# Paged keys turned by VectorE in 32x32 blocks instead of by TensorE

## The chip, the core and the metric

The kernel runs on one core of one Trainium2 chip. The metric is the device time of one execution in microseconds (us). All data is float32.

## The reference

One step of a one-layer decoder for a prompt of 512 tokens and for 64 sample tokens (8 sequences of 8). The part that matters here is the sparse attention of the sample tokens. Each sequence has 2048 past positions in 16 pages of 128 keys; a page table says where each page lies in the cache. A page of keys is `128 x 8 heads x 128` floats, 512 KB, and so is a page of values.

```python
phys = jax.vmap(lambda pt, ids: pt[ids])(page_table, pidx // PAGE_SIZE)
k_sel = jnp.where(is_past, cache_k[phys, slot], gather(k, nidx))
logits = jnp.einsum('bthd,btkhd->bthk', q, k_sel) * ATT_SCALE
logits = logits + bias                      # relative position
p = jax.nn.softmax(jnp.where(valid, logits, -inf), axis=-1)
out = jnp.einsum('bthk,btkhd->bthd', p, v_sel)
```

The kernel does not gather single keys: it computes the logits of all 2048 past keys and adds a mask that leaves the 256 chosen ones.

## The kernel before

The program is written by hand for five engines with semaphores. PE (TensorE) multiplies, ACT (ScalarE) and DVE (VectorE) empty PSUM, POOL (GpSimd) helps, and SP (SyncE) issues nearly all loads, in program order, each after the waits that stand ahead of it.

The sample attention lies in the middle of the program. It runs over two groups `G` of four sequences. For each group there are three stages.

- **Keys.** 64 pages, page number `kp` outermost and the sequence `bb` inside, so that four neighbouring pages of the loop are the same `kp` of four sequences. SP loads each page into one of eight slots `ring` (keys on the 128 partitions, 4 KB each, line 711). For the logits the head dimension must lie on the partitions, so PE turns the page by eight 128x128 transposes (line 1197) into two PSUM banks (`kp`); ACT copies one bank into `KTb` (line 1510), DVE the other (line 1793). Then PE multiplies with `QZ`, the queries of one sequence padded to 32 columns (line 1210), and adds up the four sequences in one PSUM tile `kl`. DVE adds bias and mask into `LS` (function `logits`, line 1787).
- **Softmax.** DVE and ACT finish the rows of `LS`, PE transposes the probabilities (line 1229), and they go into `PTs`.
- **Values.** 64 pages, sequence outermost, through the same eight slots; PE multiplies them as they are (line 1245).

Between these, PE computes "side" tiles, column tiles of the input projection which nothing in the attention needs: a tile is 48 matmuls (lines 987 to 989), and every second one makes SP load the next 1 MB chunk of weights, which ACT and DVE split into a high and a low part (lines 1358 and 582). Where each tile stands is set by the tables `SIDE_B`, `SIDE_V` and the calls `put_side`. Before the change: three tiles at `start`, one at each softmax, nine in each value stage, none in the key stages.

The mask of the chosen keys is computed by DVE in `S`. Ahead of the first key stage SP writes it to memory (line 719) and reads it back four times, once for each group of 32 partitions, into `MG` (line 722). These are the only large loads before the change that go to 32 partitions at a time: 32 rows of 8.5 KB each.

Of the kernel before, what the change touches and what calls it, by code (L numbers as in the profile page):

```python
# [19 lines left out]
P = 128  # L20
# [87 lines left out]
def hybrid_kernel(nc, x_prompt, x_sample, cache_k, cache_v, cache_idx_k, state_ffn_conv, page_table, rel_bias,  # L108
# [42 lines left out]
    two, three = {7: 1, 16: 1}, {4: 1, 10: 1, 16: 1}  # L151
    SIDE_V = [two, two, two, three, two, two, three, {4: 1, 10: 1}]
# [8 lines left out]
    put_side(('start',), 3)  # L161
    for G in range(2):
        put_side(('softmax', G, 0), 1)
# [59 lines left out]
    for G in range(2):  # L223
        for n in range(64):
            single.add('kp', G, n, 0)
            single.add('kp', G, n, 1)
        for kp in range(NPG):
            pair.add('kl', G, kp, at=kp % 2)
        for i, tile in enumerate(side_at['softmax', G, 0] + side_at['softmax', G, 1]):
            pair.add(*tile, at=(i + 1) % 2)  # L230
# [3 lines left out]
        for b in range(4):  # L234
            pair.add('o', G, b, at=0)
            for kp in range(NPG):
                for tile in side_at.get(('V', G, b, kp), ()):
                    pair.add(*tile, at=1)
            single.add('ot', G, b, 0)
            single.add('ot', G, b, 1)  # L240
    pair.add(*side[-1], at=1)
# [60 lines left out]
    with ctx:  # L302
# [141 lines left out]
        QZ = R3[:, 4352:6400].rearrange("p (h b c) -> p h b c", h=H, b=8)  # L444
        kTn = blocks(R3[:, 6400:7424], H)
        KTb = [blocks(RB[:, 1024 * i:1024 * i + 1024], H) for i in range(2)]
# [98 lines left out]
        def page_freed(e, seq):  # L545
# [8 lines left out]
            G, kind, n = (seq - 8) // 128, (seq - 8) // 64 % 2, (seq - 8) % 64  # L554
            if kind == 0:
                e.wait_ge(single_filled, single.slots['kp', G, n, 1][0] + 1)
            else:
                e.wait_ge(S_("v_pages_used"), 64 * G + n + 1)
# [66 lines left out]
        def _(sp):  # L625
# [78 lines left out]
            def load_page(seq):  # L704
                if seq >= 256:
                    return
                G, kind, n = seq // 128, seq // 64 % 2, seq % 64
                b, kp = (4 * G + n % 4, n // 4) if kind == 0 else (4 * G + n // 16, n % 16)
                page_freed(sp, seq)
                v = page_id(sp, b, kp)  # L710
                sp.dma_start(ring[seq % 8], (cache_k, cache_v)[kind][0, bass.ds(v, 1)]
                             .rearrange("o p h d -> (o p) (h d)")).then_inc(page_in[seq % 8], 16)

            side_loads('start')
            for seq in range(4):
                load_page(seq)

            sp.wait_ge(S_("sample_mask"), 1)
            sp.dma_start(mask_scr, S).then_inc(S_("mask_out"), 16)
            sp.wait_ge(S_("mask_out"), 16)  # L720
            for j in range(4):
# [1265 lines left out]
```

## Time and profile before

| | us |
|---|---|
| median of 3 runs (lowest, highest) | 1591.89 (1589.79, 1596.37) |
| the profiled execution: its span, first to last instruction | 1593.2 |
| first key stage, from the first transposes to the start of the softmax | 465 to 581 |
| first value stage | 596 to 705 |
| second key stage | 705 to 812 |
| second value stage | 828 to 930 |

A time of its own beside the span is not given for the profiled execution; the span lies within the range of the three runs. A stage's times are read from the timeline of the trace, and from where line 1197, 1245 or 987 begins. A duration of one matmul is longer than its share of the engine's time, since matmuls overlap in the array; so a stage's PE work is read from busy time or from the distance between repeats.

### The profile page before, as it was taken

How to read it: one execution, taken by the hardware profiler on the slowest of the kernel's cores; microseconds unless marked ns; L12 is line 12 of the kernel's file. 1: busy time of each engine (PE TensorE's matmuls, PEld its weight loads, DVE VectorE, ACT ScalarE, POOL GpSimd, SP SyncE). 2: the span in 40 equal slices, each digit the busy share in tenths (PEclk: the TensorE clock that was granted, in tenths of full speed). 3: DMA queues.
4: the chain of work that ended last, by engine and by line, in shares of the span. 5: the costliest groups of instructions: out<-in, count | busy, mean ns of one | idle time of the engine just before them, and what ended most of it. 6: DMA issues, size and time to landing. Idle time of an engine off the chain costs nothing.

```text
span 1593.2 us, 32571 instructions
## 1 busy us (share of the span) xinstructions
PE 1471.7 (92%) x13518; PEld 1334.5 (84%) x13518; DVE 762.0 (48%) x1030; ACT 511.5 (32%) x818; POOL 234.5 (15%) x371
## 2 busy tenths in 40 slices
PE   7999998979979989899998998899799999999995
PEld 4867798957867778797777998799699999999995
DVE  5288699496514540025540135543555555552123
ACT  4243223324323341023341122122344455442121
POOL 3423234154210000000000000321000110000000
PEclk8899999989999999999999999899799999999998
DMA  5415223122159979999869976133322233223221
GB/s 173 149 27 159 65 80 113 57 96 73 49 188 369 332 249 342 383 358 329 310 223 402 363 258 240 34 125 104 113 80 80 80 90 95 83 98 102 79 83 60
DMA packets 179278, 266.58 MB, mean 167 GB/s; under 512 B 20522, under 2 KB 136539, under 8 KB 178043
## 3 DMA queue, kind: packets, MB, share of 16 engines
q1 hardware_dynamic: 167947, 243.95, 44.5%
q0 software_dynamic: 5104, 11.11, 2.1%
q10 hardware_dynamic: 6080, 9.44, 1.6%
q8 instruction: 107, 1.75, 0.4%
q14 instruction: 40, 0.33, 0.1%
HBM read 240.28 MB, written 24.18 MB: 166 GB/s over the span
## 4 chain that ended last, share of the span: by engine, by line
PE 77%; DVE 8%; DMA 5%; ACT 3%; SPq 2%; issue 2%; POOL 2%; ACTq 0%; DVEq 0%
PE PS L987 14%; PE PS L989 13%; PE PS L988 13%; PE PS L1197 8%; PE PS L1210 4%; PE PS L1245 3%; PE PS L1319 3%; PE PS L1318 3%; PE PS L1317 3%; DMA R<-in_cache_v 3%; PE PS L1028 2%; PE PS L1029 2%; PE PS L1030 2%; PE PS L1173 1%; PE PS L1120 1%
## 5 line engine op out<-in xcount | busy, mean ns | idle before, releaser
L987 PE MATMUL PS<-xn_hi,WH 128*128 128x288 f32 (+1 forms) x1424 | 430.7, 302 | 16.0 <-DVE xn_lo L1614 13.2
L988 PE MATMUL PS<-xn_lo,WH 128*128 128x288 f32 (+1 forms) x1424 | 424.7, 298 | 0.0
L989 PE MATMUL PS<-xn_hi,WL 128*128 128x288 f32 (+1 forms) x1424 | 424.6, 298 | 0.0
L987 PEld LDWEIGHTS PS<-xn_hi,WH 128*128 128x128 f32 (+1 forms) x1424 | 271.1, 190 | 33.1 <-issue 22.2
L988 PEld LDWEIGHTS PS<-xn_lo,WH 128*128 128x128 f32 (+1 forms) x1424 | 271.9, 191 | 0.0
L989 PEld LDWEIGHTS PS<-xn_hi,WL 128*128 128x128 f32 (+1 forms) x1424 | 271.6, 191 | 0.0
L582 DVE TENSOR_TENSOR WL<-W,WH 128x2048 fp32r<-128x2048 f32 (+2 forms) x69 | 145.7, 2112 | 241.6 <-ACT WH L1358 241.6
L1358 ACT ACTIVATE WH<-W 128x2048 fp32r<-128x2048 f32 (+2 forms) x81 | 145.1, 1791 | 90.2 <-PE PS L1319 74.9
L1197 PE MATMUL PS<-CST,R 128*128 128x128 f32 x1024 | 142.7, 283 | 9.8 <-DMA R<-in_cache_k 9.5
L1793 DVE COPY RB<-PS 128x512 f32<-128x512 f32 x128 | 88.3, 691 | 115.7 <-PE PS L1197 115.7
L1197 PEld LDWEIGHTS PS<-CST,R 128*128 128x128 f32 x1024 | 112.1, 143 | 35.9 <-issue 25.7
L1510 ACT ACTIVATE RB<-PS 128x512 f32<-128x512 f32 x128 | 76.4, 597 | 142.7 <-PE PS L1197 142.7
L1319 PE MATMUL PS<-G_hilo,WL 128*128 128x288 f32 x352 | 103.8, 295 | 0.0
L1317 PE MATMUL PS<-G_hilo,WH 128*128 128x288 f32 x352 | 103.6, 294 | 0.0
L1318 PE MATMUL PS<-G_hilo,WH 128*128 128x288 f32 x352 | 103.6, 294 | 0.0
L1028 PE MATMUL PS<-WH,xn_hi 128*128 128x256 f32 (+1 forms) x320 | 95.4, 298 | 3.8 <-POOL WL L582 3.8
L1391 ACT ACTIVATE STG<-PS 128x576 f32<-128x576 f32 (+2 forms) x44 | 23.3, 529 | 235.0 <-PE PS L989 191.2
L1921 DVE SCALAR_TENSOR_TENSOR CV<-CV,VT 128x592 f32<-128x592 f32 x44 | 36.7, 834 | 124.4 <-ACT CV L1584 124.3
L1029 PE MATMUL PS<-WL,xn_hi 128*128 128x256 f32 (+1 forms) x320 | 91.8, 287 | 0.0
L1030 PE MATMUL PS<-WH,xn_lo 128*128 128x256 f32 (+1 forms) x320 | 91.6, 286 | 0.0
L1245 PE MATMUL PS<-R,R 128*32 128x128 f32 x2176 | 72.7, 284 | 18.1 <-DMA R<-in_cache_v 15.5
L1210 PE MATMUL PS<-RB,R 128*32 128x128 f32 x2048 | 84.4, 283 | 3.5 <-DVE RB L1793 3.5
(257 smaller groups left out, 2423.2 us busy)
## 6 DMA issues: line engine op xcount, KB each, us to landing
R<-in_cache_k SPq DMA_DIRECT2D x128, 512.0 KB, 5.3
R<-in_cache_v SPq DMA_DIRECT2D x128, 512.0 KB, 7.0
W<-in_w_in SPq DMA_DIRECT2D x30, 1024.0 KB, 5.4
W<-in_w_up SPq DMA_DIRECT2D x44, 512.0 KB, 4.6
W<-in_w_down SPq DMA_DIRECT2D x16, 704.0 KB, 4.4
x_scratch<-xT SPq DMA_DIRECT2D x2, 2304.0 KB, 9.0
W<-in_w_branch_a SPq DMA_DIRECT2D x4, 1024.0 KB, 7.9
W<-in_w_branch_b SPq DMA_DIRECT2D x4, 1024.0 KB, 6.1
```

The source lines that it names most:

```text
L582: e.tensor_tensor(WL[n % NW][:, 0:c], W[n % NW][:, 0:c], WH[n % NH][:, 0:c].bitcast(F32), ALU.subtract).then_inc(low_count[name][0], 1)
L987: pe.matmul(out, hi[:, k, cols], x.hi_block(n)[:, tokens], start=first, stop=False)
L988: pe.matmul(out, hi[:, k, cols], x.lo_block(n)[:, tokens], start=False, stop=False)
L989: return pe.matmul(out, lo[:, k, cols], x.hi_block(n)[:, tokens], start=False, stop=last)
L1028: pe.matmul(out, xn1.hi_block(k)[:, t], hi[:, k, :], start=(k == 0), stop=False)
L1029: pe.matmul(out, xn1.hi_block(k)[:, t], lo[:, k, :], start=False, stop=False)
L1197: last = pe.transpose(bank('kp', G, n, u)[:, P * i:P * i + P], ring[seq % 8][:, HD * h:HD * h + HD], ident)
L1210: last = pe.matmul(pbank('kl', G, kp)[32 * j:32 * j + 32, u, 0:P], QZ[:, h, 4 * G + bb, :], KTb[(n - 1) % 2][:, h, :], start=(bb == 0), st ...
L1317: pe.matmul(out, hi[:, k, :], gated(n, 0)[:, t], start=(n == 0), stop=False)
L1318: pe.matmul(out, hi[:, k, :], gated(n, 1)[:, t], start=False, stop=False)
L1319: last = pe.matmul(out, lo[:, k, :], gated(n, 0)[:, t], start=False, stop=(n == FB - 1))
L1358: act.activation(WH[n % NH][:, 0:c], W[n % NW][:, 0:c], ACT.Copy).then_inc(S_("high_ready"), 1)
```

## The change

A page of keys is now loaded as 32 rows of 16 KB: partition `k` of a group of 32 partitions holds the four neighbouring keys `4k` to `4k+3`. The same page number of four sequences fills the four groups of 32 partitions of `KR` (two of these, each as large as four ring slots). DVE turns it with two instructions of 2048 elements a partition in 32x32 blocks, and writes each element four words from the one before, so that the keys come out in order (`KTB`, three buffers of half a page). The partitions of `KTB` are then four sequences by 32 of the 128 head elements; `QB` holds the queries block-diagonally to match, and four matmuls with the four quarters of the head dimension add up one head's logits. ACT builds `QB` with 32 small copies.

Side tiles move: two at `start`, five in each key stage, two at each softmax, four and three in the value stages. POOL now issues the mask's store and loads. SP issues the first eight pages ahead of the load for `start`.

```diff
-    two, three = {7: 1, 16: 1}, {4: 1, 10: 1, 16: 1}
-    SIDE_V = [two, two, two, three, two, two, three, {4: 1, 10: 1}]
+    SIDE_K = [2, 5, 8, 11, 14]
+    SIDE_V = [{8: 1}, {8: 1}, {8: 1}, {8: 1}, {8: 1}, {8: 1}, {8: 1}, {}]
...
+        KR = [blocks(R1[:, 4096 * i:4096 * i + 4096], 4) for i in range(2)]
+        KTB = [a.rearrange("p (n k r) -> p n k r", n=16, r=4) for a in (RB[:, 0:2048], R3[:, 0:2048], R3[:, 2048:4096])]
...
+            if kind == 0 and n >= 8:
+                e.wait_ge(S_("k_transposed"), 32 * G + 2 * (n // 4 - 1))
+            elif kind == 0:
+                e.wait_ge(S_("v_pages_used"), 64 * G - 4 + 4 * (n // 4))
+            elif n < 8:
+                e.wait_ge(S_("k_transposed"), 32 * G + 30 + 2 * (n // 4))
...
+                    sp.dma_start(KR[kp % 2][32 * bb:32 * bb + 32, :, :],
+                                 cache_k[0, bass.ds(v, 1)].rearrange("o (k r) h d -> k (o r) (h d)", r=4))\
+                        .then_inc(page_in[seq % 8], 16)
...
+                for i in ((0, 2, 1, 3) if seq // 64 % 2 == 0 else range(4)):
+                    load_page(seq + i)
...
-                        for u in range(2):
-                            claim(pe, 'kp', G, n, u)
-                            for i in range(4):
-                                h = 4 * u + i
-                                last = pe.transpose(bank('kp', G, n, u)[:, P * i:P * i + P],
-                                                    ring[seq % 8][:, HD * h:HD * h + HD], ident)
-                            done(last, 'kp', G, n, u)
...
+                    for u in range(2):
+                        pe.wait_ge(S_("k_transposed"), 32 * G + 2 * kp + u + 1)
+                        keys = KTB[(2 * kp + u) % 3]
+                        for j in range(4):
+                            for c in range(4):
+                                last = pe.matmul(bank('kl', G, kp)[32 * c:32 * c + 32, P * u:P * u + P],
+                                                 QB[:, G, 4 * u + c, j, :],
+                                                 keys[:, 4 * c + j, :, :].rearrange("p k r -> p (k r)"),
+                                                 start=(j == 0), stop=(j == 3))
...
+                        if n in (1, 2):
+                            if G == 0:
+                                filled(dve, 'pv', H - 1)
+                            else:
+                                filled(dve, 'o', 0, 3)
...
+                        dve.transpose(KTB[n % 3].rearrange("p n k r -> p r n k"), KR[kp % 2][:, :, 512 * u:512 * u + 512]
+                                      .rearrange("p r (n d) -> p r n d", n=16))\
+                            .then_inc(S_("k_transposed"), 1)
```

On PE, at the start of the first key stage, the program had transposes out of the ring (`R_63`) and logits matmuls out of `KTb` (`RB`) in turn, eight of each for every page:

```order
L1197 MATMUL PS<-CST,R_63 128x128 x16
L1210 MATMUL PS<-RB,R_66 32x128 x8
L1197 MATMUL PS<-CST,R_63 128x128 x8
L1210 MATMUL PS<-RB,R_66 32x128 x8
L1197 MATMUL PS<-CST,R_63 128x128 x8
```

At the same place it now has, for the first three page numbers (twelve pages) and up to the first side tile inside the stage:

```order
L1213 MATMUL PS<-RB,R_66 32x128 x16
L1213 MATMUL PS<-R_66 32x128 x32
L1213 MATMUL PS<-RB,R_66 32x128 x16
L1213 MATMUL PS<-R_66 32x128 x32
L1002 MATMUL PS<-xn_hi,WH_61 128x288
L1003 MATMUL PS<-xn_lo,WH_61 128x288
```

The transposes are gone and the number of logits matmuls is the same, 32 for four pages.

On DVE, at the same place, the copies out of PSUM went ahead of the logits of the page number before:

```order
L582 TENSOR_TENSOR WL_58<-W_55,WH_62 128x2048
L1793 COPY RB<-PS 128x512 x5
L1787 SCALAR_TENSOR_TENSOR R_64<-PS,NBr,SR 128x128 x2
L1793 COPY RB<-PS 128x512 x4
L1787 SCALAR_TENSOR_TENSOR R_64<-PS,NBr,SR 128x128 x2
L1793 COPY RB<-PS 128x512 x4
```

Now six transposes stand ahead of the first logits, and the split of a weight chunk (line 589 after the change) stands among them:

```order
L589 TENSOR_TENSOR WL_60<-W_57,WH_61 128x2048
L1825 STREAM_TRANSPOSE RB<-R_63 128x4x512
L1825 STREAM_TRANSPOSE R_66<-R_63 128x4x512 x2
L1825 STREAM_TRANSPOSE RB<-R_63 128x4x512
L1825 STREAM_TRANSPOSE R_66<-R_63 128x4x512 x2
L1801 SCALAR_TENSOR_TENSOR R_64<-PS,NBr,SR 128x128 x2
L589 TENSOR_TENSOR WL_58<-W_55,WH_62 128x2048
L1825 STREAM_TRANSPOSE RB<-R_63 128x4x512
```

Four copies of 512 elements became two transposes of 2048, and ACT's four copies are gone.

On SP, the first key pages stood behind a weight load, and the mask's store and loads (`mask_scratch`) stood between the fourth and the fifth page:

```order
L711 DMA R_63<-in_cache_k 128x1024
L719 DMA mask_scratch<-SR 64x2176
L722 DMA SR<-mask_scratch 32x2176 x4
L613 TENSOR_LOAD PTAB
L613 ISA x2
L711 ISA
L711 DMA R_63<-in_cache_k 128x1024
```

Now eight pages of 32 rows are issued first, and the weight load of `start` follows the eighth:

```order
L719 DMA R_63<-in_cache_k 32x4096
L644 DMA W_56<-in_w_in 128x8x256
L620 TENSOR_LOAD PTAB
L620 ISA x2
L719 ISA
L719 DMA R_63<-in_cache_k 32x4096
```

A load that took 128 rows of 4 KB is one of 32 rows of 16 KB, and the mask no longer stands in SP's queue.

## Rows read from the trace of the kernel before

**Rows 1.** The page: busy shares, and 40 slices of the span.
```profile
PE 1471.7 (92%) x13518; PEld 1334.5 (84%) x13518; DVE 762.0 (48%) x1030; ACT 511.5 (32%) x818; POOL 234.5 (15%) x371
DMA  5415223122159979999869976133322233223221
```

**Rows 2.** Windows: stretch, length, busy us by engine, PEclk, DMA share, GB/s.
```profile
465.00:479.00 14.00, 5.69 (x80) 4.29 (x78) 2.77 (x4) 2.39 (x4) 0.00 (x0) 0.86 0.89 288
479.00:581.00 102.00, 99.93 (x1472) 76.45 (x1472) 53.29 (x94) 37.10 (x61) 0.00 (x0) 0.97 0.92 333
581.00:596.00 15.00, 10.99 (x91) 10.35 (x95) 6.27 (x14) 10.25 (x12) 2.09 (x4) 1.00 0.79 226
596.00:705.00 109.00, 98.64 (x1522) 90.06 (x1514) 13.38 (x13) 13.36 (x18) 0.00 (x0) 0.94 0.93 353
707.00:812.00 105.00, 103.11 (x1536) 79.41 (x1540) 55.11 (x95) 39.20 (x67) 0.00 (x0) 0.98 0.93 325
828.00:930.00 102.00, 95.64 (x1529) 88.69 (x1530) 13.98 (x15) 15.41 (x20) 0.00 (x0) 0.97 0.94 357
```

**Rows 3.** Timeline of PE inside the first key stage: start, us, instructions.
```profile
500.96 1.09 PE L1197 MATMUL PS<-CST,R 128*128 128x128 f32 x8
501.98 0.65 PE L1210 MATMUL PS<-RB,R 128*32 128x128 f32 x16
502.56 1.09 PE L1197 MATMUL PS<-CST,R 128*128 128x128 f32 x8
```

**Rows 4.** The page, costliest groups: busy us, mean ns, idle before.
```profile
L1245 PE MATMUL PS<-R,R 128*32 128x128 f32 x2176 | 72.7, 284 | 18.1 <-DMA R<-in_cache_v 15.5
L1210 PE MATMUL PS<-RB,R 128*32 128x128 f32 x2048 | 84.4, 283 | 3.5 <-DVE RB L1793 3.5
```

**Rows 5.** Windows of 2 us around the mask's loads, columns as in rows 2.
```profile
472.00:474.00 2.00, 0.00 (x0) 0.00 (x0) 0.00 (x0) 0.00 (x0) 0.00 (x0) 1.00 1.01 231
474.00:476.00 2.00, 0.00 (x0) 0.00 (x0) 0.00 (x0) 0.00 (x0) 0.00 (x0) 0.76 0.98 216
478.00:480.00 2.00, 1.16 (x6) 1.16 (x7) 0.00 (x0) 0.01 (x1) 0.00 (x0) 0.50 1.03 422
480.00:482.00 2.00, 2.00 (x22) 1.25 (x21) 0.80 (x2) 0.59 (x1) 0.00 (x0) 0.53 1.03 420
482.00:484.00 2.00, 2.00 (x30) 1.63 (x29) 1.19 (x3) 0.60 (x1) 0.00 (x0) 1.00 1.02 418
```

**Rows 6.** Timeline of SP's queue from 457 us on: start, us, issues.
```profile
458.31 3.79 SPq L711 DMA_DIRECT2D R<-in_cache_k  x4
462.15 0.49 SPq L719 DMA_DIRECT2D mask_scratch<-SR  x1
470.21 1.92 SPq L722 DMA_DIRECT2D SR<-mask_scratch  x4
```

**Rows 7.** Groups by shape: busy us, mean ns, idle before; DVE, then POOL.
```profile
L582 DVE TENSOR_TENSOR WL<-W,WH 128x2048 fp32r<-128x2048 f32 x52 | 119.0, 2288 | 140.8 <-ACT WH L1358 140.7
L1793 DVE COPY RB<-PS 128x512 f32<-128x512 f32 x128 | 88.3, 691 | 115.7 <-PE PS L1197 115.7
L1787 DVE SCALAR_TENSOR_TENSOR R<-PS,NBr,SR 128x128 f32<-128x128 f32 x68 | 20.5, 345 | 1.5 <-PE PS L1210 1.5
L1767 DVE TENSOR_SCALAR SR<-SR 64x2048 f32<-64x2048 f32 x1 | 1.2, 1220 | 0.0
L582 POOL TENSOR_TENSOR WL<-W,WH 128x2048 fp32r<-128x2048 f32 x12 | 55.1, 4595 | 95.0 <-ACT WH L1358 95.0
```

**Rows 8.** Timeline of ACT at the `start` tiles: the last prompt head, then drains.
```profile
444.38 0.60 ACT L1493 ACTIVATE oa<-PS 128x512 f32<-128x512 f32 x1 [2.51 <-PE PS L1173]
450.74 0.65 ACT L1391 ACTIVATE STG<-PS 128x576 f32<-128x576 f32 x1 [2.66 <-PE PS L989]
457.10 0.65 ACT L1391 ACTIVATE STG<-PS 128x576 f32<-128x576 f32 x1 [5.71 <-PE PS L989]
```

**Rows 9.** Groups by shape: POOL's large memset, ACT's small copies and its weight split.
```profile
L901 POOL MEMSET R<- 128x2048 f32 x1 | 1.8, 1813 | 0.0
L1529 ACT ACTIVATE oa<-PS 128x32 f32<-128x32 f32 x16 | 2.3, 195 | 6.2 <-PE PS L1256 3.4 <-ACT STG L1391 2.4 <-PE PS L1197 0.4
L1358 ACT ACTIVATE WH<-W 128x2048 fp32r<-128x2048 f32 x64 | 122.3, 1911 | 8.7 <-DMA W<-in_w_branch_a 5.1 <-ACT STG L1391 2.9 <-DMA W<-in_w_in 0.7
```

**Rows 10.** Windows in the value stages with the DMA engines full.
```profile
646.00:673.00 27.00, 23.10 (x356) 19.97 (x356) 2.90 (x3) 3.38 (x5) 0.00 (x0) 0.87 1.00 389
850.00:877.00 27.00, 24.06 (x368) 21.15 (x367) 2.90 (x3) 4.67 (x6) 0.00 (x0) 0.87 1.02 399
```

More of the change, by code:

```diff
@@ L160, in hybrid_kernel @@
             put_side(('B', h, i), SIDE_B[h][i])
-    put_side(('start',), 3)
+    put_side(('start',), 2)
     for G in range(2):
-        put_side(('softmax', G, 0), 1)
+        for kp in SIDE_K:
+            put_side(('K', G, kp), 1)
+        put_side(('softmax', G, 0), 2)
         put_side(('softmax', G, 1), 0)
@@ L223, in hybrid_kernel @@
     for G in range(2):
-        for n in range(64):
-            single.add('kp', G, n, 0)
-            single.add('kp', G, n, 1)
         for kp in range(NPG):
-            pair.add('kl', G, kp, at=kp % 2)
-        for i, tile in enumerate(side_at['softmax', G, 0] + side_at['softmax', G, 1]):
-            pair.add(*tile, at=(i + 1) % 2)
+            single.add('kl', G, kp)
+            for tile in side_at.get(('K', G, kp), ()):
+                pair.add(*tile)
+        for tile in side_at['softmax', G, 0] + side_at['softmax', G, 1]:
+            pair.add(*tile)
         for g in range(2):
@@ L234, in hybrid_kernel @@
         for b in range(4):
-            pair.add('o', G, b, at=0)
+            single.add('o', G, b)
             for kp in range(NPG):
                 for tile in side_at.get(('V', G, b, kp), ()):
-                    pair.add(*tile, at=1)
+                    pair.add(*tile)
             single.add('ot', G, b, 0)
             single.add('ot', G, b, 1)
-    pair.add(*side[-1], at=1)
+    for tile in side_at['end',]:
+        pair.add(*tile)
     for c in range(8):
@@ L896, in _ @@
             pool.wait_ge(S_("k_stored1"), 32)
+            pool.memset(QB, 0.0).then_inc(S_("queries_cleared"), 1)
             link(pool.memset(kTn[:, :, TS:P], 0.0))
@@ L900, in _ @@
             pool.memset(ST[0:1, 110:111], 0.0).then_inc(S_("ring_free"), 1)
-            link(pool.memset(QZ, 0.0))
-            for b in range(NB_):
-                c = b % 4
-                last = pool.tensor_copy(QZ[:, :, b, 8 * c:8 * c + 8], qT[:, :, TP + 8 * b:TP + 8 * b + 8])
-            last.then_inc(S_("sample_queries"), 1)
+            pool.wait_ge(S_("sample_mask"), 1)
+            pool.dma_start(mask_scr, S).then_inc(S_("mask_out"), 16)
+            pool.wait_ge(S_("mask_out"), 16)
+            for j in range(4):
+                pool.dma_start(MG[32 * j:32 * j + 32, :], mask_scr[0:32, :]).then_inc(S_("mask_in0"), 16)
             pool.wait_ge(S_("sample_queries"), 1)
@@ L1798, in _ @@
+                for kp in range(NPAGES):
+                    transposed(kp)
+                    if kp >= 2:
+                        logits(kp - 2)
+                    if kp == 13:
                         drained(dve, 'kl', G, 11)
                         dve.tensor_reduce(EARLY, LS[:, :, 0:12 * P], AX_X, ALU.max)
+                    splits('K', G, kp)
+                logits(14)
                 logits(15)
```

110 lines of the change are left out of this document (56 added, 54 removed).

## The prediction

> **What bounds the kernel now.** The page first: PE is busy 92% of the span, and over a third of the span, from about 460 to 960 us, the row of DMA digits stands at 6 to 9 [rows 1]. So two resources are near full exactly where the change is. The windows by stage tell which one ends last. In the key stages PE is busy 99.93 of 102 us and 103.11 of 105, the DMA engines move 333 and 325 GB/s. In the value stages PE is busy 98.64 of 109 and 95.64 of 102 us, at 353 and 357 GB/s [rows 2]. The timeline shows why PE sets the pace in the key stages: one page takes 1.60 us, from 500.96 to 502.56, and 1.02 of it are the eight transposes [rows 3]. The ceiling just above is seen where the DMA engines are full: 418 to 422 GB/s for pages of 128 rows [rows 5], 389 and 399 for longer stretches of a value stage [rows 10]. A page of 0.524 MB takes 1.25 us at 420. So dropping the transposes is worth 0.35 us a page at the most, 22 us a key stage, before the loads take over.
>
> **The transposes on PE.** They go: 64 x 1.02 = 65 us of PE work in each stage. What stays is 84.4 / 32 = 2.6 us for each four pages (a "quad") [rows 4]; five side tiles of 6.36 us each (457.10 - 450.74, [rows 8]) add 32 us a stage, 2.0 a quad. PE then has 4.6 us of work a quad, so it stops being the bound, and the stage goes at the pace of the slower of the loads and VectorE.
>
> **The loads.** A quad is 2.10 MB. Its shape is new: four loads of 32 partitions. The trace has one case of such loads, the four of the mask [rows 6]. While they run (472 to 476 us) the DMA engines count as full, 1.01 and 0.98, but move 231 and 216 GB/s; two microseconds later, with pages of 128 rows, the same full engines move 422 [rows 5]. I take the mean of the two, 223 GB/s: 9.4 us a quad, against 5.0 at 420. The change alternates the groups of partitions (0, 2, 1, 3), the mask's loads did not, and the rows are 16 KB instead of 8.5 KB; both could help, so 5.0 is the lower bound and 9.4 the upper. I take 9.4, as the mask's loads too changed over from one half of the partitions to the other without any 2 us at a higher rate. Three weight chunks a stage (1.05 MB, 2.6 us each at 400) make 0.5 us a quad more: **9.9**.
>
> The Trainium skill (SBUF — State Buffer, Door 1: The DMA port swizzle) says that 32 partitions reach 8 of 16 ports, that such loads tend to 218 GB/s against 436, and that two transfers to different halves gained only 6%; the trace agrees with its 216 to 231. By that page the alternating order would not help, and a quad would take 9.6 us instead of 9.4.
>
> **VectorE.** The block transpose has no row here. Below: 1.22 us, the fastest 2048 elements that DVE does, and 2.29 us, its usual ones; above: 4.60 us, POOL's for the same shape [rows 7]. Reads and writes of one word each cycle make 2.29 the nearest row, the step of four speaks for more; I take about 3. A quad costs DVE two transposes, two logits instructions (0.69) and a third of a split (2.29 x 2.5 / 16 = 0.36): 2T + 1.05, which is 5.6 at T = 2.29, 7 at 3, and 10.25 at 4.60 [rows 7]. Four copies of 0.69 us fall away, and ACT's, which nobody waits for. A buffer `KR` is held during its load and its transposes, with two of these and about 2 us until a load is seen: (9.9 + 2 x 3 + 2) / 2 = 9.0, so the loads stay the bound as long as T is under 4.4.
>
> **First key stage.** Before, it ran from 465 to 581 with a hole of some 8 us at 471 to 479, because the mask stood in SP's queue [rows 2, 6]. Now the first pages are issued when the last prompt head is done, 444.4 [rows 8], behind no weight load. The queries: POOL's memset 1.8 us, 32 copies of ACT at 0.2, then its split 1.9 and DVE's 2.3 [rows 7, 9]: DVE's first transpose starts at about 457, with the first quad landed. The two `start` tiles hide this on PE. The last quad's load ends at 444.5 + 16 x 9.9 = 603; landing 2, two transposes 6, last matmuls and logits 3: the softmax starts at 614 instead of 581, **+33**.
>
> **Second key stage.** Its first quad needs ring slots of value pages 56 to 59, and its loads queue behind the last value pages, so it starts about when the value stage ends: 16 x 9.9 = 158, plus landing, transposes and the end, 11, minus 1: 168 against 107 (705 to 812): **+61**. Before, eight pages stood ready here; now PE waits some 12 us at this seam, which is in the sum.
>
> **Value stages.** PE drops from 72.7 / 2 + 9 x 6.36 = 94 us to 36 + 25 and 36 + 19, far under the loads. Eight pages are in the ring at the start; 56 pages and two chunks of weights and the side tiles' stores make 32.7 MB, at 400 GB/s 82 us, against 109: -27. In the second 31.9 MB, 80 against 102: -22. Together **-49** [rows 2, 4, 10].
>
> **Softmax.** One tile more on PE, 6.36 us, of which PE's idle time there, 4.0 us of 15, hides nearly half [rows 2, 8]: **+7** for both.
>
> Sum: +33 + 61 - 49 + 7 = +52 on the span of 1593.2, which is 1.3 above the median of the runs: 1644. Each microsecond of a quad's period moves the sum by 32.
>
> **Rivals.** (1) *The alternating loads run at the full rate.* For it: each of the two halves alone explains the half rate of [rows 5], and neighbouring loads go to different halves. Against: the mask's loads passed such a change with no gain. Then a quad is 5.0 + 0.5, VectorE at T = 2.3 needs 5.65, the buffers (5.5 + 4.6 + 2) / 2 = 6.0. First stage 457 + 96 + 3 = 556, -25; second 5 + 96 + 3 = 104, -3; with -49 and +7: -70, **1522**. This is the faster side; it decides from a period of about 8.1 us down.
>
> (2) *In between*: partial overlap of the loads (290 GB/s), or full overlap and T near 3.6: a period of 8.4. +14, +39, -49, +7: +11, **1604**.
>
> (3) *VectorE becomes the bound* because a write four words on costs a second cycle an element: T = 4.60, as POOL's row. DVE 10.25 a quad, with buffers (9.9 + 9.2 + 2) / 2 = 10.6. First stage 457 + 170 + 3 = 630, +49; second 11 + 170 + 3 = 184, +77; -42: +84, **1677**; if loads and transposes interlock at the seams too, 1700. Against it: no row here has DVE slower than a cycle an element for a plain move. The Trainium skill (Vector Engine (DVE) Microarchitecture Reference, 5.2) has a step of its own for this: elements that are not in adjacent pairs cost 1.71 to 2.51 ns each where the destination steps every element. That would be 3.6 to 5.2 us for a transpose, and 1700 at its upper end. No row here shows such a write.
>
> (4) *PE at the low clock.* PE will be idle over half of a quad. After 8 us without work it was at 0.50 (1.2 GHz) and back at 1.00 within about 4 us of work [rows 5]. All at 1.2 GHz would be 9.2 us of PE work a quad, still under 9.9, so it adds a few us only; under rival 1 it would take most of the gain (1522 + 32 x 3.2 = 1624).
>
> **How the numbers follow.** Loads as the bound near 9.9: 0.40; VectorE over 10: 0.22; in between: 0.15; the full rate near 6: 0.23. The predicted time is the first's, 1644; its own range is 1630 to 1662 (a period of 9.4 to 10.4). The range 1525 to 1700 reaches from the full rate to the slow transposes. A difference under 0.5% (8 us) is about what a measurement of this kernel can't tell from none. Of the in-between cases, whose periods straddle 8.1, I give 0.06 to faster, 0.08 to the same and 0.01 to slower. Faster: 0.23 + 0.06 = 0.29; same 0.08; slower 0.40 + 0.22 + 0.01 = 0.63.
>
> **What would show it.** Right: in the key stages 4 DMAs of 32 rows land at 210 to 240 GB/s with full DMA engines, DVE waits for in_cache_k before half of its transposes, a quad every 9.9 us, PE busy under 50%; value stages of about 80 us at 390 to 400 GB/s. Wrong: over 300 GB/s in a key stage, or transposes back to back on DVE with the DMA engines idle.

## The result, and the profile after

The changed kernel takes **1707.49 us** (median of 4 runs, 1704.62 to 1712.53) against 1590.84 for the kernel before on the same chip: a ratio of **1.073**, interval 1.070 to 1.076. The prediction was 1644, its range ended at 1700. The profiled execution has a span of 1707.8 us.

The page first, rows as in [rows 1]: PE, DVE, then the digits of DMA and the GB/s of each slice.

```profile
PE 1400.2 (82%) x12494; PEld 1271.1 (74%) x12494; DVE 907.5 (53%) x966; ACT 443.9 (26%) x722; POOL 236.5 (14%) x368
PEclk8999999989966679876667988889989999999998
DMA  6323222312699989999998896714222322324231
GB/s 195 109 81 109 65 99 81 111 42 69 174 222 221 211 226 310 358 300 206 223 222 214 307 346 248 275 35 142 92 105 75 89 85 75 96 63 140 73 90 56
```

In the slices of the key stages DMA digits of 8 and 9 stand over 206 to 226 GB/s, in those of the value stages over 300 to 358: in both the engines count as full, and in the key stages they move far less. PE is busy 72 us less (130 us of work went, and the rest takes longer where the granted clock is lower) and the span grew by 115. By stage, in the columns of [rows 2] (first key stage, softmax, first value stage, second key stage, softmax, second value stage):

```profile
461.00:640.00 179.00, 94.82 (x1293) 81.37 (x1294) 137.09 (x72) 10.67 (x10) 4.86 (x12) 0.65 0.93 221
640.00:657.00 17.00, 15.39 (x119) 14.69 (x117) 6.91 (x11) 11.04 (x13) 1.37 (x3) 1.00 0.96 264
657.00:750.00 93.00, 71.81 (x1286) 58.20 (x1286) 6.56 (x9) 7.12 (x12) 0.00 (x0) 0.85 0.92 355
762.00:936.00 174.00, 93.86 (x1290) 80.54 (x1291) 134.44 (x71) 9.64 (x9) 0.00 (x0) 0.64 0.91 212
936.00:955.00 19.00, 17.33 (x182) 16.65 (x184) 8.88 (x12) 12.73 (x14) 0.00 (x0) 1.00 0.67 240
955.00:1045.00 90.00, 68.49 (x1190) 52.44 (x1178) 4.74 (x9) 4.67 (x10) 0.00 (x0) 0.81 0.90 350
```

PE is busy 53% of a key stage, at 0.64 of its clock on average; DVE 77%; the DMA engines over 90%, at 212 to 221 GB/s. The ends of the stages, against those of before plus the prediction's terms: the first key stage ends at 640, not 614 (+26); softmax and value stage take 110 us, not 100.5 (+9.5); the second key stage takes 186 us from the last value page's use, 12 of them before its first transpose, not 168 (+18); the last pair 109, not 99.5 (+9.5). That is the whole miss of 63 us, in four places.

The page's groups give the transpose: busy us, mean ns, idle before.

```profile
L1825 DVE STREAM_TRANSPOSE R<-R 128x2048 f32<-128x2048 f32 x42 | 158.4, 3807 | 57.0 <-DMA R<-in_cache_k 57.0
L1825 DVE STREAM_TRANSPOSE RB<-R 128x2048 f32<-128x2048 f32 x22 | 84.4, 3836 | 33.4 <-DMA R<-in_cache_k 31.5
```

**T, the time of one transpose, is 3.81 us**, where "about 3" was taken; VectorE's work, 2T + 1.05, is then 8.7 us a quad (four pages). DVE still waits 88.5 us for the loads, so it isn't the bound alone. Windows over one round of the buffers, columns as above:

```profile
518.00:526.00 8.00, 1.93 (x32) 1.51 (x32) 6.85 (x2) 0.00 (x0) 0.00 (x0) 0.50 1.04 228
526.00:528.00 2.00, 1.36 (x28) 1.26 (x32) 0.97 (x3) 0.00 (x0) 0.00 (x0) 0.50 0.15 33
528.00:537.00 9.00, 9.00 (x83) 8.45 (x79) 7.95 (x4) 0.48 (x1) 0.00 (x0) 0.80 1.04 229
537.00:538.00 1.00, 1.00 (x48) 1.00 (x41) 0.00 (x0) 0.51 (x2) 0.00 (x0) 1.00 0.17 33
```

and DVE's timeline beside them:

```profile
519.15 7.44 DVE L1825 STREAM_TRANSPOSE R<-R 128x2048 f32<-128x2048 f32 x2 [2.88 <-DMA R<-in_cache_k]
526.45 0.52 DVE L1801 SCALAR_TENSOR_TENSOR R<-PS,NBr,SR 128x128 f32<-128x128 f32 x2
528.84 3.90 DVE L1825 STREAM_TRANSPOSE RB<-R 128x2048 f32<-128x2048 f32 x1 [1.87 <-PE PS L1213]
532.58 3.83 DVE L1825 STREAM_TRANSPOSE R<-R 128x2048 f32<-128x2048 f32 x1
540.97 3.78 DVE L1825 STREAM_TRANSPOSE R<-R 128x2048 f32<-128x2048 f32 x1 [4.18 <-DMA R<-in_cache_k]
```

These lines show a pause: loads of 32 partitions run at 228 GB/s, then the DMA engines stand nearly empty at 526 to 528, because one buffer is full and the other was freed only at 526.5. The freed one's bytes flow from 528 to 537 and its transposes start at 540.97. So a buffer comes round in 519.15 to 540.97 = 21.8 us, two quads: 10.9. From the start of the third quad to that of the last (numbers 2 and 15, counted from 0) the period, the mean distance between quads, is 10.87 in the first key stage and 10.95 in the second, against 9.9 forecast.

### The profile page after: what moved, and what is told of

It is laid out like the page before. It is cut to its first block, busy times and chain, and to the rows that moved or that the text cites. A ratio compares the mean times of both kernels' runs of the same rounds, so it can differ in the third digit from the quotient of the medians.

```text
span 1707.8 us, 30291 instructions
## 1 busy us (share of the span) xinstructions
PE 1400.2 (82%) x12494; PEld 1271.1 (74%) x12494; DVE 907.5 (53%) x966; ACT 443.9 (26%) x722; POOL 236.5 (14%) x368
## 4 chain that ended last, share of the span: by engine, by line
PE 58%; DMA 17%; DVE 14%; SPq 4%; issue 3%; ACT 2%; POOL 1%; ACTq 0%; DVEq 0%
PE PS L1002 12%; PE PS L1004 12%; PE PS L1003 12%; DMA R<-in_cache_k 10%; DMA R<-in_cache_v 5%; DVE R L1825 5%; PE PS L1327 3%; PE PS L1326 3%; PE PS L1325 3%; DVE RB L1825 2%; SPq L620 2%; PE PS L1043 2%; PE PS L1044 2%; PE PS L1045 2%; PE PS L1252 1%
## 5 line engine op out<-in xcount | busy, mean ns | idle before, releaser
L1002 PE MATMUL PS<-xn_hi,WH 128*128 128x288 f32 (+1 forms) x1424 | 437.9, 308 | 15.2 <-DVE xn_lo L1628 13.2
L1003 PE MATMUL PS<-xn_lo,WH 128*128 128x288 f32 (+1 forms) x1424 | 430.9, 303 | 0.0
L1002 PEld LDWEIGHTS PS<-xn_hi,WH 128*128 128x128 f32 (+1 forms) x1424 | 277.7, 195 | 33.9 <-issue 23.0
L1003 PEld LDWEIGHTS PS<-xn_lo,WH 128*128 128x128 f32 (+1 forms) x1424 | 278.3, 195 | 0.0
L1825 DVE STREAM_TRANSPOSE R<-R 128x2048 f32<-128x2048 f32 x42 | 158.4, 3807 | 57.0 <-DMA R<-in_cache_k 57.0
L1213 PE MATMUL PS<-R 128*32 128x128 f32 x1344 | 73.3, 388 | 138.9 <-DVE R L1825 138.9
L1213 PEld LDWEIGHTS PS<-R 128*32 128x32 f32 x1344 | 55.7, 154 | 154.0 <-issue 118.3
L1252 PE MATMUL PS<-R,R 128*32 128x128 f32 x2176 | 90.8, 314 | 40.7 <-DMA R<-in_cache_v 35.9
L1252 PEld LDWEIGHTS PS<-R,R 128*32 128x32 f32 x2176 | 62.8, 122 | 66.7 <-DMA R<-in_cache_v 60.1
L1825 DVE STREAM_TRANSPOSE RB<-R 128x2048 f32<-128x2048 f32 x22 | 84.4, 3836 | 33.4 <-DMA R<-in_cache_k 31.5
```

The costliest lines, as they stand in the source:

```text
L1002: pe.matmul(out, hi[:, k, cols], x.hi_block(n)[:, tokens], start=first, stop=False)
L1003: pe.matmul(out, hi[:, k, cols], x.lo_block(n)[:, tokens], start=False, stop=False)
L1213: last = pe.matmul(bank('kl', G, kp)[32 * c:32 * c + 32, P * u:P * u + P], QB[:, G, 4 * u + c, j, :], keys[:, 4 * c + j, :, :].rearrange(" ...
L1252: last = pe.matmul(bank('o', G, b)[32 * j:32 * j + 32, HD * u:HD * u + HD], PTs[:, u, kp, 32 * j:32 * j + 32], page[:, HD * h:HD * h + HD] ...
L1825: dve.transpose(KTB[n % 3].rearrange("p n k r -> p r n k"), KR[kp % 2][:, :, 512 * u:512 * u + 512] .rearrange("p r (n d) -> p r n d", n=16))\
```

## The experiments

Times are medians; the kernel before had 1590 to 1594 us beside them. "Period" is as above, in the first and the second key stage. Theories A and B are those of the expectation that stands with each run. Code is shortened. For comparison, 80 us of the changed kernel's first key stage, in the columns of [rows 2], as in the experiments below:
```profile
500.00:580.00 80.00, 44.76 (x614) 38.57 (x613) 62.13 (x31) 3.86 (x4) 0.00 (x0) 0.69 0.96 218
```

**e1: the key pages over 128 partitions.** The logits are then those of other keys.
```diff
-sp.dma_start(KR[kp % 2][32 * bb:32 * bb + 32, :, :],
-             cache_k[0, bass.ds(v, 1)].rearrange("o (k r) h d -> k (o r) (h d)", r=4))
+sp.dma_start(ring[seq % 8], cache_k[0, bass.ds(v, 1)].rearrange("o p h d -> (o p) (h d)"))
```


> The changed kernel with one thing undone: each key page is loaded as 128 rows of 4 KB, as before the change, into the same bytes, so the block transposes find other keys than they should and the logits of past keys are not the reference's; every instruction and wait is the same. Theory A (the 32-partition loads and the two transposes of 3.8 us are two limits close together, which partly add because there are only two buffers): a quad falls from 10.6 to about 8.7 us, the work of VectorE, so 32 x 1.9 = 61 us less, and some 15 us less at the stage starts: about 1632 us. Rival B (VectorE's strided writes are the bound and the loads just wait for buffers): under 15 us less, 1693 to 1707.

Measured 1648.05 (ratio 1.034, 1.032 to 1.036), period 9.30 and 9.03. The same window:
```profile
500.00:580.00 80.00, 50.15 (x712) 43.59 (x716) 71.14 (x38) 5.79 (x5) 0.00 (x0) 0.69 0.76 256
```
DVE is busy 89%, the DMA engines 76%: with loads at the full rate VectorE is nearly the whole bound. The half rate costs 59 us beside slow transposes. The time is 16 us over Theory A's 1632, since the period stays 0.3 to 0.6 us over VectorE's work of 8.7.

**e2: adjacent writes.** Each transpose writes its 32 keys side by side, and the logits instruction reads PSUM with the step instead; the result is the same.
```diff
-KTB = [a.rearrange("p (n k r) -> p n k r", n=16, r=4) for a in ...]
+KTB = [a.rearrange("p (n r k) -> p n r k", n=16, r=4) for a in ...]
```


> The changed kernel with the transposes writing runs of 32 adjacent words instead of every fourth word; the order of the keys is put right when VectorE reads the logits out of PSUM (128 elements, step 32). It computes the same. If the step of four is what makes a transpose 3.8 us, it falls to 2.2 to 2.3 us; if the transpose itself is slow, it stays over 3.5. Theory A: a quad is then set by the loads alone, 9.9 us, 22 to 35 us less in all: about 1677 us. Rival B: VectorE's work falls from 8.6 to 5.6 us a quad, and the time by about 90 us, to 1617.

1681.14 (1.055, 1.052 to 1.057; Theory A), period 10.06 and 10.15. Its group on the page, then the same window:
```profile
L1828 DVE STREAM_TRANSPOSE R<-R 128x2048 f32<-128x2048 f32 x42 | 95.4, 2289 | 94.7 <-DMA R<-in_cache_k 94.7
```
```profile
500.00:580.00 80.00, 40.52 (x604) 34.12 (x600) 41.43 (x34) 3.22 (x3) 0.00 (x0) 0.71 1.02 235
```
The same shape takes 2289 ns: the step of four costs 1.52 us. DVE falls to 52%, the DMA engines to no pause (1.02), 235 GB/s. This is the prediction's main case in pure form: loads the bound, 10.1 us where 9.9 was worked out. With the step of four it took 26 us more.

**e3: both** (the logits of other keys).

> Both of the above at once (loads of 128 rows, adjacent writes; the logits of past keys are again of other keys). Theory A: neither limit is left, a quad takes about 6 us, 32 x 4.6 = 147 us less and 15 at the starts: 1545 us, or up to 1580 if TensorE's low clock takes part of it. If a third thing bounds the stage, it is above 1600.

1597.38 (1.002, 1.001 to 1.004), above its expected range of 1545 to 1580: period 7.53 and 7.19, where loads need 5.5 and DVE 5.65. A third thing is there; the part on the prediction takes it for the round of the two buffers.

**e4: the order 0, 1, 2, 3.**
```diff
-for i in ((0, 2, 1, 3) if seq // 64 % 2 == 0 else range(4)):
+for i in range(4):
```


> The changed kernel with the four loads of a quad issued in the order 0, 1, 2, 3 instead of 0, 2, 1, 3. If the alternation between the two halves of the partitions gains nothing: within 5 us of 1707. If it does gain: 10 us or more slower, with fewer GB/s in the key stages.

1715.86 (1.077, 1.074 to 1.080), period 11.00 and 11.16: 8.4 us slower by the medians, 7 by the ratios, whose intervals touch, so between the two expectations. The alternation gains little at four loads a quad.

**e5: page numbers first.** The four loads follow one another at 0.35 us instead of 1.1.
```diff
+ids = {i: page_id(sp, 4 * G + i, kp) for i in (0, 2, 1, 3)}
 for i in (0, 2, 1, 3):
     page_freed(sp, seq + i)
```


> The changed kernel, only SP reads the four page numbers of a quad into registers ahead of the waits, and issues its four loads back to back. In the changed kernel the loads are issued one every 1.1 us, so the last of a quad is issued 4.3 us after the transposes freed the buffer. Theory A, the half rate of the 32-partition loads is the bound (9.9 us a quad) and the rest comes at seams: under 10 us of difference to 1707. Theory B, a buffer's round (two transposes 7.4, issues 4.3, landing 9.9, over two buffers 10.8 us a quad) is the bound: the round loses 2 to 3 us, a quad 1.0 to 1.5, and the time falls to 1660 to 1675.

1703.39 (1.068, 1.063 to 1.073), period 10.65 and 10.89: 4 us less, which the interval can't tell from none (Theory A). At 2.3 us a load, issues of 1.1 us are hidden; Theory B's sum had counted them beside the loads.

**e6: the mask early.** POOL's mask block moves ahead of `filled(pool, 'pv', H - 1)`.

> The changed kernel, only POOL stores the sample mask and loads it back before it waits for the last prompt head, some 15 us earlier than the first key pages. Theory A: the hole of 11.4 us at the start of the first key stage (DVE idle from 476.4 to 487.8 us, waiting for the third quad) is the mask's four loads of 32 partitions in front of the pages; it goes, and the time falls by 8 to 11 us, to about 1697 to 1700. Theory B: the hole is the start-up of the two buffers themselves, and the mask takes 2 us of it at most: 1705.

1704.11 (1.069, 1.064 to 1.074), not clear of none as a time. The wait for the third quad falls from 11.37 to 6.37 us (DVE's timeline), five microseconds as the mask's 1.1 MB take at 225 GB/s; but the first transposes start 2.2 us later, at 462.8. The third quad, first in the changed kernel and then here:
```profile
487.78 7.44 DVE L1825 STREAM_TRANSPOSE R<-R 128x2048 f32<-128x2048 f32 x2 [11.37 <-DMA R<-in_cache_k]
485.57 7.45 DVE L1825 STREAM_TRANSPOSE R<-R 128x2048 f32<-128x2048 f32 x2 [6.37 <-DMA R<-in_cache_k]
```
Neither theory whole: 5 of the 11 us went with the mask, and the quad starts only 2.2 us earlier. The rest, not taken apart by a run, is the start of the buffers and the weight load of `start`, issued at 458 ahead of this quad's pages.

**e7: the side tiles where they were** (no `SIDE_K`, the old `SIDE_V`).

> The changed kernel with the side tiles where they were before the change (none in the key stages, nine in each value stage, one in each softmax, three at the start). Theory A, the value stages are bound by the loads with some PE work left uncovered, the key stages pay for three weight chunks each at the half rate: key stages -8 each, softmax -3 each, value stages +8 to +12 each: 1700 to 1710. Theory B, the value stages do not notice the tiles since the loads set their pace: -20 or more, 1685 or less. If PE bounds the value stages at its low clock, they return to 105 to 109 us each: 1715 or more.

1709.56 (1.073, 1.068 to 1.079). Periods fall to 10.15 and 10.18 without the weight chunks; softmax and value stage take 119 and 115 us instead of 110 and 109. Theory A: it comes out even.

**e8: a gather.** POOL fetches a quad in one DMA of 128 rows of 16 KB; the transposes write as in e2.
```diff
+pool.indirect_dma_start(R1[:, 4096 * (kp % 2):4096 * (kp % 2) + 4096], None,
+    cache_k[0].rearrange("n (k r) h d -> (n k) (r h d)", r=4),
+    bass.IndirectOffsetOnAxis(ap=IDX[:, 16 * G + kp:16 * G + kp + 1], axis=0))
```


> Another way to the same result: the four pages of a quad come in one gather of 128 rows of 16 KB over all partitions, issued by POOL from a table of row numbers (page times 32 plus the partition within its group), and the transposes write adjacent words as in e2. Theory A, the gather runs at the full rate like a load of 128 partitions: a quad takes 5.5 us of loads, 5.65 of DVE, and a round of a buffer (4.6 transposes, 1.5 issue, 5.5 landing, two buffers) 5.8: about 6.0, 32 x 1.2 = 38 us less than e3's 1597, so 1555 to 1570. Theory B, rows of 16 KB or the making of descriptors on POOL hold it back to 7.5 us a quad or more: 1600 or more.

1599.39 (1.002, 1.000 to 1.005). Windows in the first key stage:
```profile
500.00:504.00 4.00, 1.62 (x32) 1.51 (x32) 4.00 (x2) 0.00 (x0) 0.00 (x0) 0.54 0.86 356
504.00:505.00 1.00, 0.84 (x20) 0.49 (x16) 0.92 (x3) 0.00 (x0) 0.30 (x1) 0.50 0.88 377
505.00:506.00 1.00, 1.00 (x28) 0.90 (x20) 0.00 (x0) 0.00 (x0) 0.64 (x1) 0.50 0.16 66
506.00:510.00 4.00, 4.00 (x33) 3.65 (x26) 3.30 (x2) 0.00 (x0) 0.00 (x0) 0.85 0.95 324
```
So the same bytes in the same layout come at 324 to 377 GB/s when one DMA covers all partitions. This run changes the issuing engine and the number of loads too; e1 changes neither and also leaves the half rate. Together they say that the half rate is a matter of how many partitions a load covers, not of the rows of 16 KB. But the pause is here too (505 to 506), and the period is 7.21 and 7.35, e3's. Theory A's 6.0 is wrong with its overhead of 1.5.

**e9: the kernel before, with the mask early.**
```diff
-            sp.wait_ge(S_("sample_mask"), 1)
-            sp.dma_start(mask_scr, S).then_inc(S_("mask_out"), 16)
...
+            pool.wait_ge(S_("sample_mask"), 1)
+            pool.dma_start(mask_scr, S).then_inc(S_("mask_out"), 16)
...
             filled(pool, 'pv', H - 1)
```


> The kernel before the change, only the mask is stored and loaded back by POOL before its wait for the last prompt head, instead of by SP between key pages 3 and 4. Theory A: the hole of some 8 us at 471 to 479 us, with the mask's loads of 32 partitions in SP's queue, was a loss of its own, since PE is the bound of the key stage behind it: 5 to 9 us faster than before, a ratio of 0.994 to 0.997. Theory B: the weight chunk and the first pages would have set the start anyway: within 2 us of before.

**1581.76** (0.993, 0.991 to 0.995), the best of all: 10.6 us less than before, somewhat over Theory A's 5 to 9. The window that held the hole ([rows 2] has PE busy 5.69 of 14 us there):
```profile
465.00:475.00 10.00, 10.00 (x149) 7.74 (x148) 5.03 (x10) 3.59 (x6) 0.00 (x0) 1.00 1.03 418
```

**e10: each page in two halves.** Four heads a load, eight loads a quad, the first four as soon as the first transpose has freed its half; page numbers first.
```diff
+for u in range(2):
+    page_freed(sp, seq, u)
+    for i in (0, 2, 1, 3):
+        sp.dma_start(KR[kp % 2][32 * i:32 * i + 32, :, 512 * u:512 * u + 512], ...)
```


> The changed kernel, only each page of keys comes in two loads of four heads each (32 rows of 4 x 2 KB), the first half of a quad as soon as the first transpose has freed its half of the buffer; page numbers are read first as in e5. The transposes and their writes with a step of four stay (3.81 us). Theory A, the round of a buffer is what turns 9.9 us into the 10.9 measured: after the second transpose (7.4 us) the first bytes come 1.5 us later, the load takes 9.3 and is seen 2.3 to 3.6 later, 21 us over two buffers. With halves the loads can go on without a pause, at 9.9 to 10.1 us a quad: 25 to 30 us less than e5's 1703, 1675. Theory B, loads and transposes slow one another down in some other way (a shared port), and the period stays at 10.6 or more: 1695 or more.

1650.65 (1.037, 1.033 to 1.040), 24 us better than Theory A: period 9.08 and 9.58.
```profile
500.00:580.00 80.00, 50.41 (x720) 43.37 (x721) 76.35 (x39) 5.79 (x5) 0.00 (x0) 0.70 1.06 264
```
The window of 80 us in the first key stage shows no pause (1.06), DVE 95% busy, and 264 GB/s, more than e2 had. The gain had two causes.

**e11: e3 with halves** (the logits of other keys).

> As e3 (each key page over all 128 partitions, adjacent writes of the transposes; the logits are those of other keys), with the halves of e10. e3 had 7.2 to 7.5 us a quad although its loads need 5.0 to 5.5 and DVE 5.65. Theory A, e3 is bound by the round of its two buffers ((5.5 + 4.6 + 4.5) / 2 = 7.3): with halves it is no more, a quad takes 5.8 to 6.2, and the time falls from 1597 to 1550 to 1560. Theory B, another limit (SP's eight issues a quad at 0.35 us and more, or PE at its low clock) keeps 7 us: 1590 or more.

1582.24 (0.995, 0.993 to 0.997), period 6.85 and 7.15: between the theories by its time, Theory B's 7 us by its period. The window of 80 us, then two shorter ones inside it:
```profile
500.00:580.00 80.00, 61.48 (x917) 56.02 (x916) 59.84 (x53) 13.96 (x13) 2.02 (x4) 0.87 0.98 337
513.00:527.00 14.00, 12.04 (x158) 10.98 (x161) 12.94 (x10) 0.65 (x1) 0.00 (x0) 0.76 1.06 400
540.00:546.00 6.00, 6.00 (x46) 6.00 (x45) 3.01 (x4) 0.00 (x0) 0.00 (x0) 0.98 0.87 259
```
The first window reaches 13 us past the last transpose, so it mixes stages. The shape of the loads is not what holds the rate down: for 14 us the engines are full at 400 GB/s. Other stretches stand at 259 GB/s with a share of 0.87, here while PE computes a side tile. So the loads still stop in part, and what stops them is not settled.

**e12: no side tile in the value stages**, seven stand at the end.

> The changed kernel with no side tile in the value stages; the seven of them stand behind the attention, where PE has no idle time to hide them, so only the stages' lengths are to be compared. Theory A, the value stages took 93 and 90 us instead of 82 and 80 because a side tile keeps PE 6 to 9 us at a low clock while the ring holds eight pages, 10 us of loads, so the loads stop: the stages take 80 to 84 us each, with no stretch of 10 us under 390 GB/s. Theory B, the rate itself is lower than the 400 taken: they stay at 88 or more. The whole time is about the same or a few us more: PE work moved, 7 x 6.4 = 45 us, minus 20 of the stages: 1720 to 1735.

1721.08 (1.082, 1.078 to 1.086). For comparison, two pairs of windows of 10 us: first the changed kernel, then e12.
```profile
707.00:717.00 10.00, 7.92 (x93) 5.59 (x86) 0.00 (x0) 0.00 (x0) 0.00 (x0) 0.56 1.03 417
717.00:727.00 10.00, 9.01 (x179) 8.15 (x178) 0.61 (x2) 1.55 (x4) 0.00 (x0) 1.00 0.80 284
```
```profile
707.00:717.00 10.00, 8.40 (x130) 5.44 (x133) 0.61 (x2) 0.39 (x2) 0.00 (x0) 0.50 1.02 415
717.00:727.00 10.00, 6.55 (x152) 4.66 (x144) 0.00 (x0) 0.00 (x0) 0.00 (x0) 0.87 1.03 417
```
Softmax and value stage take 99 and 96 us instead of 110 and 109; the value stages alone some 80 and 76, at 382 and 388 GB/s. With a side tile in them the loads stop, since SP waits for pages to be used. SP's waits of the changed kernel in its first value stage (us, times, longest):
```profile
SPq L620 <- PE PS L1252: 32.9, 24, 12.5
SPq L644 <- PE PS L1004: 8.7, 2, 6.3
```
In e12 the first wait is 26.1 us, the longest also 12.5, and the second isn't there. The second is a weight load that stands in SP's queue until a side tile's matmuls are done, with pages of values behind it. So some 15 us of waits come with the tiles, in both ways. Theory A, but not all of the gain is the stops: with the tiles their weights and stores went too. The stages moved 30.6 and 29.5 MB, those of the changed kernel 33.0 and 31.5 (rates times lengths). At e12's rates these would take 86 and 81 us, an estimate; the stops are then 7 and 9 us of the 93 and 90.

**e13: e10 in the order 0, 1, 2, 3.**

> As e10, only the four loads of each half go in the order 0, 1, 2, 3 instead of 0, 2, 1, 3. e10 was faster than its own Theory A said (1651, key pages at 244 to 280 GB/s with full DMA engines, where e2 has 234 to 241). Theory A, with more and shorter loads in flight, neighbouring loads to different halves of the partitions now overlap: in this order the rate falls back to 225 to 240 GB/s and the time rises to 1665 to 1685. Theory B, the order is indifferent and the piece size or the number in flight did it: within 8 us of 1651.

1676.17 (1.052, 1.047 to 1.058), period 9.94 and 10.01:
```profile
500.00:580.00 80.00, 43.33 (x668) 36.83 (x664) 67.45 (x35) 3.77 (x4) 0.00 (x0) 0.66 1.07 238
```
Theory A: with short loads the alternation is worth 25.5 us and 26 GB/s. And against e4, the same order in whole pages, the halves gain 40 us, some 4 of them by the page numbers read first (e5): the pause is gone, at e2's rate and e2's period.

**e14: both halves wait for the whole buffer.**
```diff
-page_freed(sp, seq, u)
+page_freed(sp, seq, 1)
```


> As e10 (eight loads a quad, pieces of 2 KB), only both halves of a quad wait until the whole buffer is free, as in the changed kernel. Theory A, the round of a buffer was e10's gain: the period returns to 10.4 to 10.9 us a quad and the time to 1690 to 1703. Theory B, the pieces of 2 KB and shorter loads were the gain: the time stays within 10 us of 1651. In between, both have a share: the load of a quad at 260 GB/s takes 8.1 us instead of 9.3, a round 1.2 less, 10.0 to 10.2 us a quad and 1675 to 1685.

1654.92 (1.038, 1.033 to 1.043), period 9.34 and 9.46 at 254 and 257 GB/s: Theory B's time. The expectation took this for the end of the round as a cause, but the edit doesn't restore the round of the changed kernel: the first transpose still starts when half a quad has landed, so the round is shorter by up to a transpose at its other end.

**e15: halves, adjacent writes, mask early** (the reference's result).

> The change as it is, with what the runs pointed to: halves (e10), adjacent writes (e2), the mask early (e6); the result is the reference's. e10 is bound by VectorE (busy 95 to 99%, 8.7 us of work a quad at 3.81 us a transpose). Theory A, with 2.29 us a transpose the loads are the bound again, at 260 to 280 GB/s 7.5 to 8.3 us a quad and weights 0.5: 32 x 1.0 less than e10 and 5 for the mask, 1610 to 1625. Theory B, the rate of e10 came with the slow transposes' pacing and the loads go at 235 GB/s again: 10 us a quad, 1665 or more.

1645.60 (1.033, 1.027 to 1.039), period 8.95 and 9.02 at 263 to 270 GB/s. Between: the rate holds, but a quad with its share of weights and side tiles' stores is 2.4 MB (rate times period), 9.0 us at 266, not 8.3. The expectation took a quad without that share at that rate.

**e16: e8 with the mask early.**

> e8 (one gather of 128 rows of 16 KB a quad, adjacent writes) with the mask early as in e6; the result is the reference's. In e8 POOL issued the third quad only after the mask's round trip, and the first key stage lost about 8 us there. Theory A: 5 to 9 us less than e8's 1599, 1590 to 1594, no better than before and 10 over e9. Theory B: the start is set by the first two quads, within 2 us of e8.

1590.44 (0.999, 0.996 to 1.001): 9 us less than e8, level with before, 9 over e9. Theory A.

**e18: e2 with two loads of 8 KB rows a page.**
```diff
+for u in range(2):
+    for i in (0, 2, 1, 3):
+        sp.dma_start(KR[kp % 2][32 * i:32 * i + 32, 2 * u:2 * u + 2, :], ...)
```


> As e2 (adjacent writes, each transpose after the whole quad has landed, 1681), only each page comes in two loads of 32 rows of 8 KB, eight loads a quad in the order 0, 2, 1, 3 and again, with the page numbers read first. Theory A, the number of loads lets those to different halves overlap, whatever their pieces: 254 to 270 GB/s as in e10, 9.0 to 9.3 us a quad instead of 10.1, 1645 to 1660. Theory B, it was the 2 KB pieces of e10: 235 GB/s as e2, within 8 us of 1681, or 1675.

1649.76 (1.038, 1.037 to 1.040), the page numbers again read first; period 8.93 and 9.28:
```profile
500.00:580.00 80.00, 48.61 (x720) 41.74 (x720) 48.29 (x38) 5.77 (x5) 0.00 (x0) 0.75 1.00 269
```
Theory A: the pieces of 2 KB are not needed, eight shorter loads in alternating order are enough, 269 GB/s against e2's 235.

## Why the prediction was wrong

**What held.** The direction, and the main mechanism. "I take 9.4", the half rate of loads of 32 partitions at 223 GB/s, was right: 228 and 229 in the windows above, 9.2 us a quad, and a period of 10.1 with weights where nothing else interferes (e2). That 9.9 came so near has a little luck in it: the side tiles' stores were left out (e2's 235 GB/s times 10.06 us is 2.36 MB a quad, where 2.10 and three chunks make 2.29), and the rate was a little better. The rival (1) of full-rate loads falls with it: only loads over all partitions reach that rate (e1, e3, e8). That the alternating order would not help held for four loads a quad, 7 or 8 us, and not for eight: 238 against 264 GB/s (e13, e10). The seam before the second key stage was 11.7 us, some 12 forecast. Softmax with two tiles: 17 and 19 us, where 18.5 and 19.5 were forecast.

**The step that failed first: "I take about 3" for T.** Bounds 2.29 and 4.60 were right, the choice between them not; it is 3.81, and e2 prices it at 26 us. DVE waits 88 us for loads in the key stages, so this should have cost nothing by the prediction's own rule ("the loads stay the bound as long as T is under 4.4"). That 4.4 is where VectorE's work reaches 9.9; the prediction's own buffer term reaches it at T = 3.95 already, still above 3.81.

**The step that made it cost, and failed with it: the buffer's term, (9.9 + 2 x 3 + 2) / 2.** Its 2 us "until a load is seen" is mis-sized: with T = 3.81 the term still gives 9.75, no cost. Measured in the changed kernel's round: 1.5 us from the last transpose's end to the first bytes (526.5 to 528), and 2.0 to 3.8 us from a load's last bytes (they end at 517.2, 526.5 and 537.2) to the transposes that read it, of which PE, at 0.50 of its clock and holding the third transposed buffer, has a part once (the 1.87 above). With 4.5 in place of 2 the term fits the two corners that it bounds, D being a quad's loads with weights:

```
             D      2T    (D + 2T + 4.5)/2   other bound    period measured
after        9.9    7.6        11.0          9.9 loads      10.9
e1           5.5    7.6         8.8          8.7 VectorE    9.0 to 9.3
e2           9.9    4.6         9.5          9.9 loads      10.1
e3, e8       5.5    4.6         7.3          5.65 VectorE   7.2 to 7.5
```

The 4.5 is fitted to these traces, not measured by itself. Two of the rows fix it; e1 lies 0.2 to 0.5 us above both bounds, and e2 is bound by its loads. What stands behind the round as a cause is the pause in the lines above, and as a test e13 against e4: the loads split, with the order kept, the pause gone, 40 us. That test also lets the first transpose start after half a quad, which shortens the round as well. e14 does not decide against it, but no run changes the latencies alone. The DMA engines' 0.93 and 0.91 of the key stages hid it, since a share over 90% reads as full. So the rival (3) was the nearest in time (1677, "if loads and transposes interlock at the seams too, 1700"), by its second half: not VectorE as the bound, but loads and transposes taking turns. The rule of the Trainium skill beside it (Vector Engine (DVE) Microarchitecture Reference, 5.2, 1.71 to 2.51 ns an element) agrees by its range: 3807 / 2048 = 1.86 ns, and adjacent writes give 1.12. Its figures are for other instructions and for longer steps than four words.

**"Together -49" for the value stages: 21 us too much.** The sum took 400 GB/s throughout and PE "far under the loads". A sum over the stage was the wrong measure: each side tile keeps PE 6.6 to 8.0 us in one piece (its clock had fallen before the longer ones, 0.56 above) and the ring holds 10 us of pages, so the loads stop, the more as SP also waits at a weight load for a tile's end (8.7 us in the first value stage), and they come back no faster than 417. The stages took 93 and 90 us where 82 and 80 were forecast. By the estimate of e12 7 and 9 us of that are the stops; the rest is a mean rate of 382 and 388 GB/s even without tiles.

**The first key stage's start: 12 us in e2.** "The last quad's load ends at 444.5 + 16 x 9.9" lets the loads run on from the first; but quads 2 and 3 need buffers that the first transposes free at 468, and the mask's 5 us and the weight load of `start` stand before them. e2, free of the slow T, starts its third quad at 486.4, where 444.5 + 3 x 9.9 + 2 = 476.2 was implied, and ends this stage at 626 where 614 was forecast. The mask was read in [rows 6] for its rate, and not charged where it had moved to.

The sum, from the traces: 29 (T and the round: the key stages end at 640 and take 186 us, in e2 626 and 171; the medians of the two kernels give 26) + 19 (value stages 21, softmax -2) + 12 (start) + 3 (the second key stage of e2: 171 us, 168 forecast) = 63, the miss.

**PE's clock**, rival (4), adds little in the key stages as said: PE at 0.50 waits there. In the value stages it lengthens three of the seven side tiles from 6.6 to 7.5 and 8.0 us, where no step looked.

**Where the gain went.** 130 us of PE work were removed, and PE was the bound by only 22 us a stage at the full rate. The layout that removes the work halves the load rate (59 us beside slow transposes), writes with a step (26), and couples VectorE with the loads through two buffers. Repaired one by one (e15, e18; e16 for the gather) it comes to 1646, 1650 and 1590, the last level with the kernel before. What beats both kernels is e9, the kernel before without its mask in SP's queue, 1582.

**Still open:** why two shorter loads a page overlap across the halves and one whole load hardly does; why e11's period stays at 6.9 to 7.2 us though its loads reach 400 GB/s; and a third buffer, which would test the round directly, has not been tried for want of space.

## What to carry to other kernels

A chain of load, work and release over two buffers has a period of half its whole round, with every latency at its ends; price it with the time from issue to the first byte and from the last byte to the consumer, before comparing bandwidths and busy times. When a stage is forecast from its sum, look at the largest single piece in it against what the buffers hold: a side tile of 6.6 to 8.0 us against 10 us of pages stopped the loads that the sum had running. And a small helper transfer found in a queue (the mask) was worth more than the redesign: moving it gave 0.7%.

## What the runs showed of the hardware

- A block transpose of 128x2048 float32 on VectorE takes 2.29 us with adjacent writes and 3.81 with writes four words apart.
- Loads of 32 partitions: 228 GB/s by themselves. With the weights' share in the window, four a quad 232 to 235 (e2), eight a quad 236 to 238 in the order 0, 1, 2, 3 and 254 to 270 in the order 0, 2, 1, 3, whether the pieces are 2 or 8 KB. The alternation paid 7 to 8 us at four loads a quad, barely clear of noise, and 25 at eight.
- One gather of 128 rows of 16 KB by POOL costs POOL 0.94 us and runs at 324 to 377 GB/s.
- The DMA share says nothing of the bytes: 1.02 to 1.07 stood beside 235, 238, 264 and 417 GB/s.
